# Rows of an expert turn by indirect DMA, fetched a turn ahead and added in DRAM, instead of one-hot matrix products

## The reference

```
def moe_swiglu(h, router, w_gate, w_up, w_down):        # h: 512 tokens x 1024, 8 experts of width 3584, top 2
    logits = t @ router
    top_v, top_i = top_k(logits, 2);  gates = softmax(top_v)
    ...                                                 # tokens sorted by expert, in blocks
    def run_block(args):
        tok, e = args
        return (silu(t[tok] @ w_gate[e]) * (t[tok] @ w_up[e])) @ w_down[e]
    out = map(run_block, ...) * slot_g[:, None]
    y = zeros_like(t).at[slot_tok].add(out)
x = x + moe_swiglu(rmsnorm(x, norm_ffn), ...)
out = rmsnorm(x, final_norm)
```

## Time and profile before

| | us |
|---|---|
| median of 3 runs (lowest, highest) | 2807.58 (2803.63, 2822.59) |
| span of the profiled execution | 2817.3 |
| its own time, the longest of the three, the only one above its span | 2822.59 |
| routing ends, the first weights are asked for | 1404 |
| first matmul of the first split turn | 1422 |
| five split turns | to 2170 |
| three plain turns | to 2797 |
| TensorE busy, of the span | 2571.8 (91%) |

### The profile page before, as it was taken

How to read it: one execution, slowest core, us unless ns; L and a number is a source line. 1 busy time by engine, 2 the same in 40 slices (tenths; PEclk the granted TensorE clock), 3 DMA queues, 4 the chain that set the end, 5 groups by cost and what they waited for, 6 DMA issues and landing times.

```text
span 2817.3 us, 43050 instructions
## 1 busy us (share of the span) xinstructions
PE 2571.8 (91%) x17909; PEld 2228.2 (79%) x17909; DVE 1247.4 (44%) x1583; ACT 919.5 (33%) x1210; POOL 38.1 (1%) x110
## 2 busy tenths in 40 slices
PE   7999889999989777778689998989899999999996
PEld 5966688888878666647688897979798997996995
DVE  3344442333253667443378686868686001001001
ACT  3244222222232333243166574747474000000001
POOL 5000000000000000000000000000000000000000
PEclk9999589999999888889699999999999999997998
DMA  5300012232221000010099696969696884882660
GB/s 167 104 16 1 30 56 95 90 123 97 85 89 57 2 2 2 17 45 1 24 348 361 221 360 220 362 220 361 220 361 209 269 269 153 268 267 87 228 224 30
DMA packets 328450, 432.31 MB, mean 153 GB/s; under 512 B 7375, under 2 KB 290870, under 8 KB 328270
## 3 DMA queue, kind: packets, MB, share of 16 engines
q1 hardware_dynamic: 327150, 427.37, 45.1%
q0 software_dynamic: 1120, 2.20, 0.3%
HBM read 427.43 MB, written 2.12 MB: 152 GB/s over the span
## 4 chain that ended last, share of the span: by engine, by line
PE 86%; DVE 7%; ACT 3%; issue 3%; DMA 1%; SPq 0%; DVEq 0%; ACTq 0%
PE bank L595 83%; PE bank L598 3%; DVE arena L1628 2%; DVE slot L1628 1%; ACT w_high L1550 1%; DVE w_low L1628 1%; ACT arena L1281 0%; DVE arena L1655 0%; DMA slot<-in_moe_w_gate_dram 0%; DVE small L1677 0%; DVE xs L1628 0%; DVE xg_low L1628 0%; DMA xs<-in_x_dram 0%; ACT arena L1451 0%; ACT arena L1328 0%
## 5 line engine op out<-in xcount | busy, mean ns | idle before, releaser
L595 PE MATMUL bank<-arena 128*128 128x144 f32 (+9 forms) x3584 | 587.3, 324 | 29.1 <-DVE arena L2117 16.6
L595 PEld LDWEIGHTS bank<-arena 128*128 128x128 f32 (+3 forms) x3584 | 459.7, 191 | 121.6 <-issue 75.3
L1628 DVE TENSOR_TENSOR w_low<-slot,w_high 128x2048 fp32r<-128x2048 f32 x172 | 394.2, 2292 | 321.7 <-ACT w_high L1262 274.4
L595 PE MATMUL bank<-w_high,xg_high 128*128 128x256 f32 x1120 | 324.7, 290 | 17.2 <-issue 9.1
L595 PE MATMUL bank<-w_low,xg_high 128*128 128x256 f32 x1120 | 319.4, 285 | 0.0
L595 PE MATMUL bank<-w_high,xg_low 128*128 128x256 f32 x1120 | 319.0, 285 | 0.0
L595 PE MATMUL bank<-arena,slot 128*128 128x144 f32 (+3 forms) x2304 | 298.2, 312 | 14.8 <-ACT slot L1472 14.8
L595 PEld LDWEIGHTS bank<-arena,slot 128*128 128x128 f32 (+2 forms) x2304 | 284.7, 193 | 28.0 <-ACT slot L1472 16.0
L1628 DVE TENSOR_TENSOR arena<-arena,bank 128x256 f32<-128x256 f32 (+3 forms) x134 | 64.0, 477 | 527.2 <-PE bank L595 527.2
L1628 DVE TENSOR_TENSOR w_low<-arena,w_high 128x2048 fp32r<-128x2048 f32 x105 | 240.7, 2292 | 64.3 <-ACT w_high L1550 64.3
L595 PE MATMUL bank<-h_high,w_high 128*128 128x512 f32 x592 | 236.9, 400 | 7.7 <-DVE h_low L1628 7.7
(11 more groups left out here) (317 smaller groups left out, 3404.8 us busy)
## 6 DMA issues: line engine op xcount, KB each, us to landing
slot<-in_moe_w_gate_dram SPq DMA_DIRECT2D x64, 1024.0 KB, 6.2
arena<-in_moe_w_down_dram SPq DMA_DIRECT2D x64, 1024.0 KB, 6.1
slot<-in_moe_w_up_dram SPq DMA_DIRECT2D x56, 1024.0 KB, 6.8
arena<-in_moe_w_up_dram SPq DMA_DIRECT2D x56, 1024.0 KB, 6.7
arena<-in_moe_w_gate_dram SPq DMA_DIRECT2D x48, 1024.0 KB, 6.0
slot<-in_moe_w_down_dram SPq DMA_DIRECT2D x48, 1024.0 KB, 6.6
slot<-in_e_w_in_dram SPq DMA_DIRECT2D x12, 1024.0 KB, 5.3
slot<-in_ff_w_gate_dram SPq DMA_DIRECT2D x11, 1024.0 KB, 5.2
```

The source lines that it names most:

```text
L595: return pe.matmul(o, lhsT, rhs, start=start, stop=True, skip_group_check=True)
L1628: return dve.tensor_tensor(o, a, b, op)
```

## The change

The normalized rows and the residual go to DRAM (`h_d`, `sum_d`, 512 rows and CAP spare rows of zeros). `pick` x (token number, gate), 8 matmuls with two columns, gives each slot its token's row number and gate (`slot_rows`, `slots_to_rows`; an empty slot gets a spare row). GpSimd fetches the next turn's rows by indirect DMA (`gather` there), TensorE transposes them in three steps through acc[3] (`turn_rows`), in the middle of the turn. The outputs, scaled by the gate as they leave PSUM, are added to `sum_d` by an indirect DMA with addition (`add_rows`), while the next turn runs. At the end sum_d is loaded back and the result stored tile by tile. pick_g, pickT, the gather and scatter products, `scattered` and the wait moe_done go. Hidden rows turn through acc[2] alone. The waits of the ring, the banks and the loops are redone to match. The core of the diff:

```diff
+        h_d = nc.dram_tensor("h_rows_d", [SEQ + CAP, D], F32)
+        sum_d = nc.dram_tensor("sum_rows_d", [SEQ + CAP, D], F32)
@@ SyncE, before the turns, and after them
+                sp.wait_ge(sem("x_added"), 40)
+                for t in range(NT):
+                    sp.dma_start(sum_d[P * t:P * (t + 1), :], xs[:, t, :]).then_inc(sem("h_stored"), 16)
+                for t in range(NT):
+                    sp.wait_ge(sem("xn_ready"), 3 * NT + t + 1)
+                    sp.dma_start(h_d[P * t:P * (t + 1), :], xn[:, t, :]).then_inc(sem("h_stored"), 16)
...
-                sp.wait_ge(sem("y_ready"), NT)
-                sp.dma_start(out[0].rearrange("(t p) d -> p t d", p=P), y_out).then_inc(sem("stored"), 16)
+                sp.wait_ge(sem("summed"), total("summed", ends[2] * 32))
+                for t in range(NT):
+                    sp.dma_start(xs[:, t, :], sum_d[P * t:P * (t + 1), :]).then_inc(sem(f"x_back{t}"), 16)
...
+                for t in range(NT):
+                    sp.wait_ge(sem("y_ready"), t + 1)
+                    sp.dma_start(outv[:, t, :], y_out[:, t, :]).then_inc(sem("stored"), 16)
@@ GpSimd, constants (zero rows stored to the spare rows) and, new, its loop
+                def gather(turn, ahead, cap):
+                        pool.wait_ge(sem("idx_ready"), total("idx_ready", turn + (ahead + 1)))
...
+                        pool.tensor_tensor(spare_mark[:, 0:1], ones[:, 0:1], ones[:, 0:1], ALU.mult).then_inc(sem("pool_mark"), 1)
+                        pool.indirect_dma_start(xg_tok[:, 0, :], None, h_d[:, :], bass.IndirectOffsetOnAxis(ap=idx_ahead[:, 0:1], axis=0))\
+                            .then_inc(sem("xg_landed"), 16)
+                        n = cap - P
+                        pool.indirect_dma_start(xg_tok[0:n, 1, :], None, h_d[:, :], bass.IndirectOffsetOnAxis(ap=idx_ahead[0:n, 1:2], axis=0))\
+                            .then_inc(sem("xg_landed"), 16)
+                def add_rows(turn, cap):
+                        pool.wait_ge(sem("out_tok_ready"), turn * 4 + 8)
+                        pool.wait_ge(sem("rows_taken"), total("rows_taken", turn + 1))
+                        pool.wait_ge(sem("summed"), total("summed", turn * 32))
...
+                        pool.indirect_dma_start(sum_d[:, :], bass.IndirectOffsetOnAxis(ap=idx_now[:, 0:1], axis=0), out_tok[:, 0, :], None,
+                                                compute_op=ALU.add).then_inc(sem("summed"), 16)
...
+                        gather(turn, 1, next_cap)
+                        add_rows(turn, cap)
@@ TensorE
+                def slot_rows(turn, ahead, cap):
                         pe.wait_ge(sem("pick_ready"), turn + (ahead + 1))
...
+                            m = mm(acc[3][:, 0:2], pick[:, t, 0:P], slot_vals[:, t, :], t == 0)
+                        for t in range(NT):
+                            m = mm(acc[3][0:cap - P, 2:4], pick[:, t, P:cap], slot_vals[:, t, :], t == 0)
+                        m.then_inc(sem("idx_full"), 1)
+                def turn_rows(turn, ahead, cap, i):
+                        if i == 0:
...
+                            pe.wait_ge(sem("xg_landed"), total("xg_landed", turn * 32 + 32 * (ahead + 1)))
+                        else:
+                            pe.wait_ge(sem("xg_ready"), turn * 3 + (3 * ahead + i))
+                        for d in range(3 * i, min(3 * i + 3, KT)):
+                            tp(acc[3][:, CAP * (d % 3):CAP * (d % 3) + P], xg_tok[:, 0, P * d:P * (d + 1)])
+                            m = tp(acc[3][:, CAP * (d % 3) + P:CAP * (d % 3) + cap], xg_tok[0:cap - P, 1, P * d:P * (d + 1)], cap - P)
@@ TensorE, expert_split
+                        rows_after = {16: 0, 19: 1, 22: 2}
...
-                        turn_tokens(turn, P, CAPS[1])
-                        scatter(turn, P)
+                            if n == 10:
+                                slot_rows(turn, 1, CAPS[1])
+                            if n in rows_after:
+                                turn_rows(turn, 1, CAPS[1], rows_after[n])
@@ ScalarE, expert_split
+                            if n == TILES_E - 3:
+                                act.wait_ge(sem("up_full"), turn * GROUPS_E + (FF_TILES + GROUPS_E))
+                                xg_parts(turn, 1)
...
-                            if n < TILES_E - 1:
+                            if n < TILES_E - 2:
                                 high(turn, ring, n + SPLIT)
+                        high(turn, ring, TILES_E - 2 + SPLIT)
                         act.wait_ge(sem("down_used"), turn * GROUPS_E + (10 + GROUPS_E))
...
+                        act.activation(out_tok[:, 0, 0:512], acc[0][:, :], ACT.Copy, scale=gate_now[:, 0:1]).then_inc(sem("out_tok_ready"), 2)
                         high(turn, ring, TILES_E - 1 + SPLIT)
-                        xg_parts(turn, 1)
@@ VectorE, expert_split (its first call, gates, goes)
+                            if n == TILES_E - 3:
+                                xg_parts(turn, 1)
+                            if n == 7:
+                                rows_now(turn, P)
+                                place_slots(turn, 1, CAPS[1])
+                            if n == 11:
+                                slots_to_rows(turn, 1, CAPS[1])
+                            if n in rows_after:
+                                gathered(turn, 1, CAPS[1], xgT, rows_after[n])
...
-                            if n < TILES_E - 1:
+                            if n < TILES_E - 3:
                                 low(turn, n + SPLIT)
-                        gathered(turn, 1, CAPS[1])
+                        low(turn, TILES_E - 3 + SPLIT)
+                        low(turn, TILES_E - 2 + SPLIT)
+                        dve.wait_ge(sem("down_used"), turn * GROUPS_E + (10 + GROUPS_E))
...
+                        dve.tensor_scalar(out_tok[:, 0, 512:], acc[1][:, :], gate_now[:, 0:1], None, ALU.mult).then_inc(sem("out_tok_ready"), 2)
                         low(turn, TILES_E - 1 + SPLIT)
-                        xg_parts(turn, 1)
-                        scattered(turn)
```

More of the change, by code:

```diff
@@ L391, in pair_of @@
             return view.rearrange("p (a b) -> p a b", b=CAP)[:, :, 0:cap]
-        landed = [sem(f"landed{i}") for i in range(SLOTS)]
+        landed = [sem(f"landed{i}") for i in range(RAW)]
         block = ctx.enter_context(nc.Block())
@@ L1081, in _ @@
                 ends = [pe.value_load(turn_ends_i[0:1, i:i + 1], min_val=i + 1, max_val=MAX_TURNS) for i in range(len(CAPS))]
-                def gather(turn, ahead, cap):
+                def slot_rows(turn, ahead, cap):
                         pe.wait_ge(sem("pick_ready"), turn + (ahead + 1))
-                        for i in range(3):
-                            b = turn_banks[1 + i]
-                            for d in range(3 * i, min(3 * i + 3, KT)):
-                                for t in range(NT):
-                                    m = mm(b[:, CAP * (d % 3):CAP * (d % 3) + cap], xn[:, t, P * d:P * (d + 1)], pick[:, t, 0:cap],
-                                           d % 3 == 0 and t == 0)
-                            m.then_inc(sem("xg_full"), 1)
@@ L1596, in expert @@
                                 .then_inc(sem("sil_ready"), 1)
+                        act.wait_ge(sem("up_full"), turn * GROUPS_E + (FF_TILES + GROUPS_E))
+                        act.wait_ge(sem("xg_ready"), turn * 3 + 6)
+                        act.activation(xgT[:, 0:4, :], xg_ahead[:, 0:4, :], ACT.Copy).then_inc(sem("xg_copied"), 1)
                         act.wait_ge(sem("down_used"), turn * GROUPS_E + (10 + GROUPS_E))
-                        for i in range(3):
+                        for i in (0, 2):
                             n = min(3, KT - 3 * i)
@@ L1601, in expert @@
                                 .then_inc(sem("outT_ready"), 1)
-                        gates_turned(turn, cap)
-                        for i in range(4):
+                        act.wait_ge(sem("rows_taken"), total("rows_taken", turn + 1))
+                        act.wait_ge(sem("summed"), total("summed", turn * 32))
+                        for i in (0, 2):
                             act.wait_ge(sem("out_tok_full"), turn * 4 + (i + 1))
@@ L1618, in _ @@
                     expert(turn, CAPS[2])
-                act.wait_ge(sem("moe_done"), 1)
                 norm(4)
```

213 lines of the change are left out of this document (125 added, 88 removed).

## The result

The changed kernel takes 2677.3 us (median of 4 runs, 2674.9 to 2683.3); the kernel before, run beside it, 2806.9 (2803.6 to 2822.6). The ratio is 0.951, 95% interval 0.948 to 0.954. The forecast was 2667, with a range of 2642 to 2722. Between the two profiled executions, on which the sum was made, the difference is 2822.59 - 2677.68 = 144.9 us, against 154.7 in the sum. Against the median of the kernel before the difference is 129.6, against 141.5 in the forecast.

The account below looks back on a forecast made before the run. TensorE, busy 91% of the span, was taken as the bound, with serial work in each turn's tail. Terms summed to -154.7 us: 2667.9 from the profiled 2822.59, 2666.1 by the median; 2667 given, range 2642 to 2722.

Parts of the forecast that it names:

- R1: Rival, late rows: a gather takes 20 us instead of 8, TensorE stands before tile 17; +54, 2721 us; chance 0.10.
- R2: Rival, contention in the split loop: GpSimd or the additions' reads delay w_low or weights; +25, 2692 us; chance 0.14.
- R3: Rival: gathered and added rows go one by one; at 40 us a transfer the kernel takes 2891 us; chance 0.04.
- R4: Rival: VectorE's insertion hidden, both clock drops vanish, head no later; 2646 us; chance 0.10.
- (a): Split turn's end: TensorE's work after the last down tile goes; 16.8 us saved a turn, 83.9 in five.
- (d): Branch back of the split loop: 0.9 us saved four times, 1.5 added after the fifth turn; 2.1 saved together.
- (b): Before the last down tile of split turns: wait for hid_low falls from 4.50 to 1.2 us; 16.5 saved in all.
- (c): Last down tile of split turns runs at full clock after the shorter wait; 1.66 us saved a turn, 8.3 in all.
- (e): Slow first gate tile after the split loop's branch costs 2.0 us four times; half counted, 4.0 saved.
- (f): Added on TensorE mid-turn: 8 two-column matmuls and 16 transposes; 2.9 us in each of eight turns, 23.2 added.
- (g): VectorE's added work at n = 7 of split turns: 4.0 us, 2.1 reaching TensorE; 10.5 added in five turns.
- (h): GpSimd's gathers, additions and marks beside VectorE in split turns: 1.0 us a turn taken, 5.0 added.

Follow-up runs that it names:

- the run with 16 rows: Changed kernel with the loops' 128-row indirect DMAs (gather and addition) moving only 16 rows; ratio 0.948 to the kernel before, split turns 132.4 to 133.9 us.
- the old kernel with the new order: Kernel before, with only the weights' split for the next turn's tiles moved behind the last hidden tile; ratio 0.9885, turns 143.3 to 144.1 us.
- the four extra picks: Changed kernel with four more unused one-hot rows on VectorE at the seventh tile of each split turn; turns 133.3 to 134.7 us.
- the transposes apart: Changed kernel with each group's three wide row transposes done before its three narrow ones; ratio 0.948 to the kernel before, turns 133.2 to 135.9 us.
- the last two variants: Changed kernel with loop-head code prefetched (2661.6 us), and that plus wide transposes before narrow and index and gate copies moved to the fourth tile (2647.6 us).
- the hint: Changed kernel with TensorE's turn loops told to fetch the loop head's code ahead of the branch back; 2661.6 us against 2674.2 beside it.

## Why the prediction was right, and where its terms were off

The reading held: the tail of a turn was serial work on the bounding engine, and cutting it counted whole; no rival came true. R1 (late rows) failed for want of lateness: from GpSimd's mark at 1603.22 to the landing of the second gather (6.1 us after its issue, by the median) it is 8.1 us, against 8 taken, and the room was 12.9 us, against 11.5. R2 is excluded by the run with 16 rows, as far as the rows' bytes go, and by the groups of tiles in a turn that hold no inserted work: seven of them, measured from down tile to down tile, take 8.71 to 8.74 us, as before. R3 falls with the same landing. R4 named two things that happened in part (a cheap insertion, fast first gate tiles). By the terms, per split turn where nothing else is said:

- (a) and (d) together, over the five turns: 86.0 forecast, 82.5 measured. At the four branches 19.1 us between the last down tile and the next gate tile became 2.4 to 2.8, and the fifth turn has no pause before or after.
- (b) 3.3 forecast; the wait is 0.93, so 3.6. (c) 1.66 forecast, 1.56 measured (4.46 to 2.90). Taken by experiment the edit is worth 6.1 to 6.4, since it also brings most of (e).
- (e) was misread first: between 1722.30 and 1727.12 lie 27 matmuls, not 24. From its first start to its last end the slow tile took 4.62 us, a fast one 3.10, so it cost 1.5 us and not 2.0 (the same slip is in R4). "Whether 1.5 us of idle still lowers the clock" was also only half of the question: in the old kernel with the new order the pause at the branch stayed at 1.9 to 2.4 us and the tile ran in 3.1 to 3.9, so most of the slowness came with the old order. After, the tile takes 3.10 us at three of the four branches and 4.49 at one: 1.2 us a turn saved, 1.0 forecast. A price that was too high and only half of it counted nearly cancel. What picks the slow one stays open: with 16 rows the tile was slow behind pauses of 2.14 and 2.22 us and fast behind 2.34 and 2.18.
- (f) Undersized: "2.9 us in each of the eight turns". Slot rows took 1.2 us instead of 0.93, and the transposes 1.3, 1.3 and 0.9 on top of their groups, 3.5 instead of 1.97: 4.7 in all, 14 us more over eight turns. I had priced 16 transposes by a row in which all were wide; here wide and narrow alternate, and apart they take 0.77 instead of 1.27 for six.
- (g) Oversized: forecast 2.1, measured 0.7 of waiting. The insertion took 2.5 us (VectorE's timeline, below), not 4.0, since the small operations follow one another in 0.06 us. The working (a slack of 1.94, the rest paid in full) was right, as the four extra picks showed.

```profile
1589.30 0.15 DVE L2193 COPY gate_now<-gate_ahead 128x1 f32<-128x1 f32 x1
...
1590.54 0.23 DVE L2169 TENSOR_SCALAR arena<-arena,turn_off 128x4 f32 x1 [0.91 <-DVE spare_mark L2198]
...
1591.77 2.28 DVE L1685 TENSOR_TENSOR w_low<-arena,w_high 128x2048 fp32r<-128x2048 f32 x1
```

- (h) 1.0 forecast, nothing measured.
- Branch back, in (d) and the plain tails: the size was wrong; the branch was named as the cause, but not the fetch of code that it waits for. "About 4.3 us from the last instruction it can issue", less the queued work, gave 1.5 and 2.3; it was 2.3 to 2.7 and 4.4. The way round is longer than 4.3 us and not fixed: 5.3 to 5.7 us from the start of the last down tile, 6.4 from the start of the sixteen transposes, 5.9 to 7.6 with the transposes apart. In the kernel before the pause was 2.2 to 2.4 us, so this part of (d) saved nothing. Conversely, where a loop ends there was no pause at all (2445.50 follows the transposes directly), where I had added 1.5 once and 2.3 once.
- Plain tails: first 5.5 forecast, 7.3 measured (0.92 + 2.0 + 4.4), and 2.9 us more in the gate tile behind it; second 5.5 forecast, 2.7 measured. With some 5 us of the rows in each these are the -15.0 and, within 1.2 us, the -37.2 above.
- End: 33.9 forecast, 33.3 measured, with the last addition at 8.2 instead of 7.5. Head: 1.7 forecast, 3.2 measured.

The sum of 154.7 was made on the spans and what lies around them; that last part shrank by 3.2 us (5.3 to 2.1), so of the spans the sum is 13.0 short. By stage, with 2.9 us of (f) in each turn as forecast: 3.5 are the stretch before the routing, which no step touches; 1.5 the head; 1.1 the split loop (84.8 forecast, 83.7 measured); 2.3 the rows in the first plain turn (5.2 instead of 2.9); 7.0 the first plain tail, its slow gate tile and the rows behind it (22.0 forecast, 15.0 measured). Against them stand 1.9 for the second plain tail (35.3 forecast, 37.2 measured) and 0.5 for the end.

That the split loop, the bulk of the gain, came out within 1.1 us is luck in part. Five turns were short by 9.0 us in (f), 3.5 in (a) and (d) and 0.5 in (c), and better than forecast by 7.0 in (g), 5.0 in (h), 1.4 in (b) and 0.7 in (e). These cancel; some 2 us are left, most of them 0.15 us beside each of the two insertions.

What stays open: the pause at the branch goes with the last transfer of code, but why that comes later in one turn or program than in another (2.3 to 2.7 us of pause in the changed kernel, 2.2 to 2.9 in its second profile, 2.9 to 4.6 with the transposes apart) is not shown; nor is what makes one first gate tile slow and the next one fast; and how much of the 2.1 us a turn between the last two variants belongs to the transposes and how much to the moved copies, which were not run apart.

## What to carry to other kernels

Products whose only work is to move rows can go to an indirect DMA wherever the rows are known some 10 us ahead; what they cost then is their transposes and the small work that makes the indices, so place that by the slack of each engine. When an edit on the path brings nothing, look for the pause that grew in its stead, here the branch back of TensorE's loop. And take an order of work apart from the transfer it comes with: a quarter of this change's gain was such an order.

## What the runs showed of the hardware

- The way back to the head of a long loop (900 matmuls) cost TensorE pauses of 1.2 to 4.6 us with nothing late (2.3 to 2.7 in the changed kernel), 4.4 to 4.7 behind sixteen short transposes, and with the hint 0.7 to 1.5 in the split loop and none in the plain one. Each pause ended 1.7 to 2.1 us after a 16 KB transfer of the kind "instruction". The Trainium skill ("Advanced Engine Details and Errata", Control Flow Timing) gives about 108 ns for a compare-and-branch; most of the pauses here are twenty to forty times that, so it does not cover a head that must be fetched. Its section "ISA Cache" describes instructions held in lines of 16 KB; the size of the transfers here agrees, though no run here varied the size of the loop.
- A pause of TensorE of about 4 us costs more than itself: 4.4 us of waiting lengthened a turn by about 7, with a mean granted clock of 0.73 in the 10 us behind it, so partly at 1.2 GHz instead of 2.4; in the turn of the changed kernel shown above, waits of 0.68 and 0.93 us and a pause of 2.32 left the mean granted clock at 1.00.
- Issuing an indirect DMA took GpSimd 0.9 to 3.6 us, nearly whatever the number of rows (3.31 with 16, 3.60 with 128), about twice as long where it started during a w_low of VectorE (1.97 against 0.96, 3.60 against 1.63, 2.39 against 1.34), which itself took 2.29 us as ever; a gather landed some 6 us after its issue (4.0 to 7.4), and the last addition and its signal took 8.2 us, 7.0 with 16 rows.
